# Lower shift and scale in two quarters, first two feed-forward units interleaved, nine half units parked

## The reference, cut to what matters

```python
cond = jax.nn.silu(c)
for i in range(DEPTH):
    mod = jnp.einsum('bd,sdk->bsk', cond, ada_w[i]) + ada_b[i]
    shift_t, scale_t, gate_t = jnp.split(mod[:, 0], 3, axis=-1)
    shift_m, scale_m, gate_m = jnp.split(mod[:, 1], 3, axis=-1)
    h = modulate(rmsnorm(x, norm_g[i, 0]), shift_t, scale_t)
    ...
    x = x + gate_t[:, None, :] * y
    h = modulate(rmsnorm(x, norm_g[i, 1]), shift_m, scale_m)
    x = x + gate_m[:, None, :] * sq_relu_mlp(h, mlp_w1[i], mlp_w2[i])
return rmsnorm(x, final_g)
```

## Time and profile before

| | |
|---|---|
| median of 3 runs | 2360.92 us |
| lowest, highest | 2359.98, 2361.58 us |
| span of the profiled execution | 2356.4 us |
| what lies outside the span, by the three runs | 3.6 to 5.2 us |
| PE busy, PEld busy | 2263.7 us (96%), 1826.6 us (78%) |
| DVE, ACT, POOL busy | 71%, 46%, 4% |

### The profile page before, as it was taken

One profiled execution on the slowest core, in us unless ns is written; L12 is line 12 of the kernel. 1 busy time (PEld: TensorE's weight loads), 2 busy tenths in 40 slices (PEclk: granted clock), 3 DMA queues, 4 the chain that ended last, 5 costly groups with the idle time before them and its releaser, 6 DMA issues.

```text
span 2356.4 us, 28624 instructions
## 1 busy us (share of the span) xinstructions
PE 2263.7 (96%) x10121; PEld 1826.6 (78%) x10121; DVE 1667.1 (71%) x1796; ACT 1083.2 (46%) x1340; POOL 103.2 (4%) x183
## 2 busy tenths in 40 slices
PE   5489999999999998999999999999999999999998
PEld 2147788888888887888888888887888888888887
DVE  4668888888887889767667767667877555555556
ACT  2324554544534545444444444444553453443453
POOL 0000000100100001001000001000000000000000
PEclk9699999999999999999999999999999999999999
DMA  9999988998988977867667867766897766766764
GB/s 401 415 413 399 330 300 327 373 339 273 364 303 313 343 250 248 289 222 266 217 232 234 284 220 243 258 210 211 324 339 248 241 206 196 225 211 191 231 203 154
DMA packets 272172, 650.74 MB, mean 276 GB/s; under 512 B 20712, under 2 KB 21144, under 8 KB 264992
## 3 DMA queue, kind: packets, MB, share of 16 engines
q1 hardware_dynamic: 260320, 611.92, 74.7%
q0 software_dynamic: 10816, 36.24, 4.5%
q10 hardware_dynamic: 896, 0.75, 0.1%
HBM read 631.49 MB, written 17.33 MB: 275 GB/s over the span
## 4 chain that ended last, share of the span: by engine, by line
PE 85%; DVE 4%; DMA 3%; issue 1%; ACT 1%; POOL 0%; POOLq 0%; SPq 0%; DVEq 0%; ACTq 0%
PE acc L670 83%; DMA raw<-in_mlp_w 3%; DVE w_lo L1497 1%; PE tb L785 1%; PE acc L1052 1%; ACT w_hi L1102 0%; PE score_ps L1039 0%; DMA scratch<-in_decay 0%; DVE ada_acc L1503 0%; DVE h_lo L1753 0%; DVE ev L1799 0%; PE score_ps L845 0%; DVE seg_row L1586 0%; PE tb L919 0%; DVE ada_acc L1584 0%
## 5 line engine op out<-in xcount | busy, mean ns | idle before, releaser
L1497 DVE TENSOR_TENSOR w_lo<-raw,w_hi 128x1024 fp32r<-128x1024 f32 x775 | 943.9, 1223 | 591.0 <-ACT w_hi L1102 587.4
L1102 ACT ACTIVATE w_hi<-raw 128x1024 fp32r<-128x1024 f32 x775 | 821.8, 1061 | 1118.0 <-PE acc L670 984.6
L670 PE MATMUL acc<-w_hi,h_lo 128*128 128x512 f32 x1788 | 699.2, 391 | 3.7 <-issue 1.6
L670 PE MATMUL acc<-w_hi,h_hi 128*128 128x512 f32 x1788 | 696.2, 389 | 0.0
L670 PE MATMUL acc<-w_lo,h_hi 128*128 128x512 f32 x1788 | 695.8, 389 | 0.0
L670 PE MATMUL acc<-w_hi,a_lo 128*128 128x512 f32 x1312 | 513.4, 391 | 5.6 <-DVE w_lo L1497 5.6
L670 PE MATMUL acc<-w_lo,a_hi 128*128 128x512 f32 x1312 | 511.4, 390 | 0.0
L670 PE MATMUL acc<-w_hi,a_hi 128*128 128x512 f32 x1312 | 511.4, 390 | 0.0
L670 PEld LDWEIGHTS acc<-w_hi,h_lo 128*128 128x128 f32 x1788 | 335.7, 188 | 76.8 <-issue 5.5
L670 PEld LDWEIGHTS acc<-w_hi,h_hi 128*128 128x128 f32 x1788 | 335.6, 188 | 70.0
L670 PEld LDWEIGHTS acc<-w_lo,h_hi 128*128 128x128 f32 x1788 | 335.8, 188 | 68.6
(11 more groups left out here) (193 smaller groups left out, 925.7 us busy)
## 6 DMA issues: line engine op xcount, KB each, us to landing
raw<-in_mlp_w SPq DMA_DIRECT2D x512, 512.0 KB, 4.9
ada_raw<-in_ada_w SPq DMA_DIRECT2D x248, 512.0 KB, 6.4
raw<-in_ret_w_in SPq DMA_DIRECT2D x192, 512.0 KB, 4.6
ada_early_h<-in_ada_w SPq DMA_DIRECT2D x32, 1024.0 KB, 13.1
raw<-in_ret_w_out SPq DMA_DIRECT2D x64, 512.0 KB, 4.3
ada_raw<-in_ada_w SPq DMA_DIRECT2D x16, 1024.0 KB, 12.3
square_blocks<-ev POOLq DMA_DIRECT2D x84, 128.0 KB, 5.1
ev<-square_blocks POOLq DMA_DIRECT2D x21, 512.0 KB, 6.2
```

Source lines behind the costliest of these rows:

```text
L670: mm = nc.tensor.matmul(acc[pair][t][:], l[:, CK * c + j, tok], w[:, c % RING, j, :], start=first and j == 0 and i == 0, stop=last and j = ...
L1102: nc.scalar.activation(w_hi[:, o % RING], raw[:, o % RING], ACT.Copy).then_inc(hi_ready, 1)
L1497: nc.vector.tensor_tensor(w_lo[:, o % RING], raw[:, o % RING], w_hi[:, o % RING].bitcast(F32), ALU.subtract).then_inc(lo_ready, 1)
```

## The change

1. Segment 3 comes in another order: its first 16 pieces hold shift and scale together for columns 0 to 511 (quarter 0), its last 16 the same for columns 512 to 1023 (quarter 1). A piece still has 512 KB, now as two runs of 2 KB in each row of the source where it was one of 4 KB. Quarter 0 is summed in `score_ps`, quarter 1 in `mod_ps`; each has its own copy, column and gain.
2. The first two half units are run interleaved: chunks 0 and 1 of unit 0, chunks 0 and 1 of unit 1 (all four need quarter 0 only), then chunks 2 and 3 of each. Between the first four stand PE's quarter-1 pieces, the fills 4 to 7, and the column of quarter 1.
3. `first_gate` stands ahead of PE's pieces of segment 3.
4. Nine half units are parked instead of eight; group (0, 3) begins with the upper half of the ninth. The piece counts of segment 4 between chunks are moved to suit.

```diff
-PARTS = 8
+PARTS = 9
-HALVES = {(0, 0): (0, 1, 2, 3), (0, 1): (4, 5), (0, 2): (6, 7)}
+HALVES = {(0, 0): (0, 1, 2, 3), (0, 1): (4, 5), (0, 2): (6, 7), (0, 3): (8,)}
+PAIRED = ((0, 0), (0, 1), (1, 0), (1, 1), (0, 2), (0, 3), (1, 2), (1, 3))
-    return 0 if j < RING else min(SEG, 4 + 6 * (j - RING) // 5)
+    return 0 if j < len(PAIRED) else min(SEG, 6 + 6 * (j - len(PAIRED)) // 5)
```

On SP:

```diff
+            pair_behind = {14: (0,), 15: (1,), 17: (2,), 19: (3,), 28: (4,), 30: (5,), 31: (6, 7)}
             for a in range(SEG):
                 load_early(3, a)
-                if a == 30:
-                    load_chunk(0, first_part(0))
+                for s in pair_behind.get(a, ()):
+                    i, c = PAIRED[s]
+                    load_chunk(s, pair_rows[i](c))
```

On PE:

```diff
-            shared_rows(3, 0, 4)
             first_gate()
-            shared_rows(3, 4, 16)
+            shared_rows(3, 0, 12)
             pe.wait_ge(gate_ready, 4)
             pe.wait_ge(diag_ready, 1)
-            for f in range(KT // 2 - 1):
-                norm_fill(f)
-                if f in (1, 3):
-                    shared_rows(3, 15 + f, 17 + f)
-                elif f == 5:
-                    shared_rows(3, 20, 28)
-            shared_rows(3, 28, SEG)
+            norm_fill(0)
+            norm_fill(1)
+            shared_rows(3, 12, 14)
+            norm_fill(2)
+            norm_fill(3)
+            shared_rows(3, 14, KT)
             column(score_ps)
-            norm_fill(KT // 2 - 1)
+            paired_units({0: [lambda: shared_rows(3, 16, 20)],
+                          1: [lambda: norm_fill(4), lambda: norm_fill(5), lambda: shared_rows(3, 20, 24)],
+                          2: [lambda: norm_fill(6), lambda: norm_fill(7), lambda: shared_rows(3, 24, 28)],
+                          3: [lambda: shared_rows(3, 28, SEG), lambda: column(mod_ps)]})
```

On DVE:

```diff
-            early(3, 8, 11)
             gated(2)
             gated(3)
-            early(3, 11, 16)
+            early(3, 8, 11)
             mean_square()
-            early(3, 16, 18)
             diagonals()
-            early(3, 18, SEG)
+            early(3, 11, KT)
             lo(0)
             second_hi()
             second_lo(0)
-            take_half(0)
+            take_quarter(0)
...
             second_lo(1)
+            early(3, 16, 18)
+            lo(2)
+            early(3, 18, 21)
+            lo(3)
+            early(3, 21, SEG)
+            lo(4)
+            lo(5)
+            take_quarter(1)
+            gains(slice(4, 8))
             split_h(2)
```

More of the change, by code:

```diff
@@ L519, in load_early @@
                     return
-                norm, part, half = (0, seg, a // KT) if seg < 3 else (1, a // KT, seg - 3)
                 slot, to = early_slot(seg, a)
-                sp.dma_start(to, ada_flat[norm, a % KT * P:(a % KT + 1) * P, part,
-                                          half * AW:(half + 1) * AW]).then_inc(ada_in[slot], 16)
+                here = slice(a % KT * P, (a % KT + 1) * P)
+                if seg == 3:
+                    q = a // KT
+                    sp.dma_start(to.rearrange("p (j n) -> p j n", j=2),
+                                 ada_flat[1, here, 0:2, q * NB:(q + 1) * NB]).then_inc(ada_in[slot], 16)
+                else:
+                    sp.dma_start(to, ada_flat[1, here, a // KT, AW:D]).then_inc(ada_in[slot], 16)
             def load_ada(seg, a):
@@ L662, in _, with chunk @@
             n = Count()
-            def chunk(c, lhs_hi, lhs_lo, pair, first, last, tiles=range(TT)):
+            def chunk(c, lhs_hi, lhs_lo, pair, first, last, tiles=range(TT), slot=None):
+                slot = c % RING if slot is None else slot
                 for j in range(CK):
@@ L702, in first_chunk, with half_unit @@
                         tok = slice(t * P, (t + 1) * P)
-                        mm = nc.tensor.matmul(acc[0][t][:], h_lo[:, j, tok], w_hi[:, 0, j, :], start=False, stop=False)
+                        mm = nc.tensor.matmul(acc[bank_pair(0)][t][:], h_lo[:, j, tok], w_hi[:, 0, j, :], start=False, stop=False)
                 mm.then_inc(w_used, 1)
-            def half_unit(kind, pair, after, c0, free, very_first=False):
+            def paired_units(after):
[3 more added lines that the diff above has]
+                        pe.wait_ge(evac, 4 * TT)
+                        first_chunk()
+                    else:
+                        ready_h(c)
+                        chunk(c, h_hi, h_lo, bank_pair(i), c == 0, c == HALF - 1, slot=s % RING)
+                    for hook in after.get(s, []):
+                        hook()
+                n.unit("p1")
+                n.unit("p1")
+            def half_unit(kind, pair, after, c0, free):
                 for o in range(HALF):
@@ L712, in half_unit @@
                         free()
[L713 to L717, removed]
+                    ready_h(c0 + o)
+                    chunk(c0 + o, h_hi, h_lo, pair, o == 0, o == HALF - 1)
                     for hook in after.get(o, []):
@@ L1305, in _ @@
             n.add(XA=4, U=2)
-            for f in range(KT // 2 - 1):
+            for f in range(4):
                 transposed_x(f)
             hi(0)
-            copy_rows(score_ps, 2, PE_BEFORE[4 * SEG])
+            copy_rows(score_ps, 1, PE_BEFORE[QUARTER_1], 0, 2)
             norm_second()
             norm_bank(1)
-            norm_bank(2)
             act.wait_ge(hi_ready, n.n["U"] * HALF + 2)
             hi(2)
-            norm_bank(3)
-            hi(3)
-            transposed_x(KT // 2 - 1)
-            for i in range(PARTS):
+            hi(3)
+            transposed_x(4)
+            transposed_x(5)
+            hi(4)
+            transposed_x(6)
+            transposed_x(7)
+            hi(5)
+            copy_rows(mod_ps, 1, PE_BEFORE[4 * SEG], 2, 4)
+            norm_bank(2)
+            norm_bank(3)
+            hi(6)
+            hi(7)
+            for s, (i, c) in enumerate(PAIRED):
+                if s >= RING:
+                    hi(s + LEAD)
+                if c == HALF - 1:
+                    act.wait_ge(w_used, n.n["U"] * HALF + s + 1)
+                    for t in range(TT):
+                        nc.scalar.activation(part_tile(i, t), acc[bank_pair(i)][t][:], ACT.Copy).then_inc(evac, 1)
+            n.unit("p1")
+            n.unit("p1")
+            for i in range(2, PARTS):
                 for s in range(HALF):
@@ L1326, in _ @@
                 for t in range(TT):
-                    nc.scalar.activation(part_tile(i, t), acc[i % 2][t][:], ACT.Copy).then_inc(evac, 1)
+                    nc.scalar.activation(part_tile(i, t), acc[bank_pair(i)][t][:], ACT.Copy).then_inc(evac, 1)
                 n.unit("p1")
@@ L2023, in _ @@
             second_lo(1)
+            early(3, 16, 18)
[7 more added lines that the diff above has]
+            gains(slice(4, 8))
             split_h(2)
-            lo(2)
             split_h(3)
-            lo(3)
-            for i in range(PARTS):
+            lo(6)
+            lo(7)
+            for s in range(RING, len(PAIRED)):
+                early(4, late_summed(s + LEAD - 1), late_summed(s + LEAD))
+                lo(s + LEAD)
+            n.unit("p1")
+            n.unit("p1")
+            for i in range(2, PARTS):
                 for s in range(HALF):
```

75 lines of the change are left out of this document (43 added, 32 removed).

## The result

| | before | changed |
|---|---|---|
| median of 12 runs each, same chip | 2359.79 us | 2365.15 us |
| lowest, highest | 2358.43, 2361.84 | 2363.64, 2366.65 |
| span of the profiled execution | 2356.4 us | 2364.1 us |

The ratio is 1.0023 with a 95% interval of 1.0015 to 1.0031: 5.4 us slower, between 3.5 and 7.3 us. The forecast was 2368.0 in a range of 2359 to 2373, slower by 6.9 us.

A forecast was written before the change was run, and what follows sets the result against it. The prediction took PE to bound the kernel behind the start. PE 5.9 us behind at the fifth chunk, less 1.4 for the last wait, plus 2.4 for low clock, made 6.9 us slower: 2368 us, range 2359 to 2373.

The forecast's parts named there:

- What bounds the kernel: Behind the start the kernel waits for PE, busy 60 of 60 us from 200 to 260, so only PE's lost time counts.
- the rival of the loads: Start phase: the stream of loads was the real limit, so the change is 8.3 us faster, 2352.6; chance 0.12.
- Gate first and the first fill: Ahead of the first fill: gating starts 1.84 us earlier, the fill stands at 166.0 not 169.37, PE idles 5.4 us.
- The first chunk: First chunk's matmul, behind the first column: starts at 179.1, 8.6 us earlier than before, with a 2.4 us idle time.
- The fifth chunk: Behind the second column: starts at 204.5, where it was 198.6, after a 2.9 us path; PE is 5.9 us behind.
- The clock: Low clock behind the idle times at both columns: second in full, first by half, 2.4 us lost; bounds 0 and 3.2.
- The total: Whole kernel: 5.9 - 1.4 + 2.4 = 6.9 us slower; 4.5 of it without the clock.
- DVE beside it: Before the second column: DVE's ten pieces and two low parts end at 196.4, PE wants them at 197.5; costed at nothing.
- The last wait: PE's wait for the last piece of segment 4: all 1.4 us taken back; bounds 0 and 1.4.
- 2 KB runs: Loads of segment 3: 391 GB/s against 398, 2%, landing 0.8 us later, under the slack; no cost counted.
- the first rival: At the columns: no low clock and shorter seams, 4.5 down to 2.5 us slower, 2363.4 to 2365.4; chance 0.25.
- The base: From span to median: the span lies 4.5 us below the median of the runs, so 2363.3 becomes 2367.8.

The follow-up runs named there:

- e2: The changed kernel with fills 4 and 5 moved right behind the first column, ahead of the first chunk; 2364.17 us, ratio 1.0017 to the kernel before.
- e8: The kernel before with nine half units parked instead of eight and nothing else of the change; 2358.58 us, ratio 0.9995.
- e1: The changed kernel with PE's last quarter-1 pieces and the second column ahead of chunk 1 of unit 1; 2362.72 us, ratio 1.0015 to the kernel before.
- e5: As e3, with DVE summing pieces 16 and 18 of segment 3 ahead of chunk 0's low part; 2360.58 us, ratio 1.0003 to the kernel before.
- e6: As e5, with PE's pieces 12 and 13 moved back ahead of the first fill; 2357.97 us, ratio 0.9998 to the kernel before.
- e3: The changed kernel with the edits of e1 and e2 together; 2362.2 us, ratio 1.0012 to the kernel before.
- e4: The kernel before with the gate row ahead of PE's first two pieces of segment 3, nothing else of the change; 2359.2 us, ratio 0.9999.
- e7: As e6, with piece 21 moved from DVE to PE; 2359.32 us, ratio 1.0001 to the kernel before.

## Why the prediction was right, point by point

- **What bounds the kernel: half wrong.** I read "PE busy all 60 us" as a start that waits for PE alone, and held that against the rival of the loads. The gate-first kernel shows that PE's place in that stretch is set by loads: 2.9 us won ahead of it are gone by 187.65. A busy PE and a full DMA can both be read in one window, and the chain tells which leads. It did no harm to the sign, since the changed kernel is late on PE by more than the loads leave.
- **Gate first and the first fill: right.** I put the first fill 16.2 us behind the pooling end, with 5.4 of idle time; it stood 15.6 behind, with 5.08.
- **The first chunk: right.** 29.3 us behind the pooling end by the sum, 28.4 measured, and the wait ahead of it 2.1 for 2.4.
- **The fifth chunk: right.** 204.5 by the sum, 204.71 measured; ACT's copy 0.74 for 0.75, the wait ahead of it 2.9 for 2.9. That last hit is in part luck, as 2.9 was picked between bounds of 1.3 and 3.3. The pooling end was 1.4 us earlier than in the kernel before, so the way to the fifth chunk was 1.6 us longer than I had it. That is the clock behind the first column, which the sum to this point leaves out.
- **The clock: the mis-sized term.** I counted the second column's stretch in full and the first by half, 2.4 us. Both fell. The first cost 4.6 - 3.0 = 1.6, by the first chunk here and in e2; the second 48.13 - 46.52 = 1.6. Together 3.2, the upper bound that I gave.
- **The total: closer than its terms, by luck.** The idle time grew by 3.8 us and not by 4.5, the clock cost 3.2 and not 2.4. The two errors nearly cancel: 7.0 for 6.9. The stretch grew by 7.4; the last 0.4 is not placed.
- **DVE beside it: right, with more margin than I gave it.** Its pieces ended at 194.06 and PE's sums began at 197.63, so 3.6 us and not 1; the ten pieces and two low parts took 14.6 us as summed, but began 2.4 earlier than I had it. The 10.3 us of the earlier trace rows are a median and not the most that a load takes, as I read them; DVE waited for no load there. With PE 4.8 us earlier and DVE 1.4 later, 6.2 against 3.6, the wait of 2.7 was there.
- **The last wait: right.** All of the 1.4 was taken back; the kernel before with nine parked units alone gets 1.1.
- **2 KB runs: nothing on the path, but 5% and not 2%.** The chain of the changed kernel has no load in it from 140 to 291. In the window 166:168 the changed kernel moves 386 GB/s and the gate-first kernel, with 4 KB runs, 408:

```profile
166.00:168.00 2.00, 2.00 (x11) 1.63 (x12) 0.00 (x0) 0.88 (x2) 0.00 (x0) 0.66 1.05 386
```

```profile
166.00:168.00 2.00, 2.00 (x11) 0.95 (x8) 1.16 (x1) 0.00 (x0) 0.00 (x0) 0.65 1.02 408
```

  It is the direction that the Trainium skill gives (Perfetto Trace Analysis, "DMA Optimizations"), by a twentieth and not dramatic. From 150 to 175 us it is 387 against 408.
- **The rival of the loads: its mechanism is there, its price was not.** I gave it 8.3 us, 10.9 of PE's chunks against 2.6 of loads (its neighbour, the first rival, should have gone down to 2.9 and not 2.5 slower, by its own bound of 1.3). With PE's delays nearly gone, the point is 283.57: 1.5 us earlier than before. DVE's last sum of segment 4 ends at 279.06, where it ended at 269.62 before, 9.4 later and not 2.6. I had counted two chunks of loads ahead of the last piece and overlooked that in DVE's written order it stands four chunks further back (`late_summed` starts from chunk 8 and not 4). DVE has them to do first, at 2.6 us a chunk and piece.
- **The rest of the kernel is not the same in every execution.** The profiled spans differ by 7.7 us and the points at 285 by 6.0. Of the other 1.7, 1.1 lie near 908 us, behind the retention of the first layer, which the change does not touch; the rest comes later. Windows of the changed kernel there:

```profile
908.00:910.00 2.00, 2.00 (x5) 1.62 (x6) 1.93 (x6) 1.76 (x6) 0.16 (x1) 0.52 0.75 272
910.00:912.00 2.00, 2.00 (x7) 1.53 (x6) 1.99 (x5) 0.00 (x0) 0.39 (x1) 0.63 0.86 236
```

  PE waits there in every kernel, first for 1.9 us, 3 us later for up to 1.3, and then for some 0.36, 0.33 and 0.80. The clock fell behind the later ones in the changed kernel, e2 and e8, behind the 1.9 in e1, e5 and e6, and not at all in before, e3, e4 and e7. In e5 it stays down from 892 to 899, and its span lies 5.4 above before's where its median lies 1.4 above. So the table's "between" compares the edits better than the spans do.
- **The base was off by 2.7 us.** I took what lies outside the span as 4.5, from the median of three runs. In every run since it is 1.8 or 1.9; the profiled execution was simply one of the kernel's faster ones. In 33 executions the kernel before has 20 spans from 2356.2 to 2357.4 and 13 from 2358.5 to 2362.0; in 34 others they lie from 2355.8 to 2359.9 without such a gap. Of the 2.9 us by which the predicted median was too high, 1.5 are the difference (6.9 for 5.4) and 1.1 the median of before, 2360.9 of three runs against 2359.8 of twelve; the rest is rounding. Against the stretch the sum was 0.5 too low.

**What stays open.** Why the medians show 5.4 us where the stretch shows 7.4. A part can be worked out: an early end of the pooling product gives the kernel before nothing (gate first), but a PE-bound start gains by it, so an execution of before with an end at 148.5 would read 136.5 between and not 135.2. That leaves 6.1, inside the interval of 3.5 to 7.3. No version beats the kernel before by what these runs can tell; the intervals of e4 to e8 all hold 1. The lowest runs of e5 to e8 are 2356.87, 2357.27, 2356.97 and 2356.95, against 2358.03 for the lowest of the 33 of before beside them, but 2357.59 was the lowest of before beside e1 to e4. So the 1.1 to 1.5 us by which e6, e7 and e8 reach the point at 285 earlier are read from one trace each and not shown in the times.

## What to carry to other kernels

When a stage is cut in two so that its first half can start earlier, the way from the last sum to the first product (copy, column, bias, modulation, split) is paid once for each half, and PE must have work to lay over each of them: one chunk or two fills behind the column took back 3.4 to 4.7 us here, more than half of it idle time and the rest clock. Price a new idle time of 2 us on PE together with the low clock that may stand behind it, 1.6 us a time in this kernel. And before an engine that is 100% busy is called the bound, make it earlier by a microsecond in one small edit and see if a later point moves.

## What the runs showed of the hardware

- The same idle time does not always bring the clock down. Behind 2.30 us of idle time near 141 us the window 142:144 shows 0.54 in the kernel before and 0.50 in e1, e2 and e5, but 1.00 in the six others, behind 2.28 to 2.67 us. The timelines and windows of e5 and e7:

```profile
140.98 1.94 PE L823 MATMUL mod_ps<-ada_acc,ones 128*32 128x512 f32 x8 [2.30 <-DVE ada_acc L1552]
```

```profile
142.00:144.00 2.00, 2.00 (x16) 0.23 (x8) 0.00 (x0) 0.00 (x0) 0.00 (x0) 0.50 1.05 386
```

```profile
140.89 1.07 PE L823 MATMUL mod_ps<-ada_acc,ones 128*32 128x512 f32 x8 [2.30 <-DVE ada_acc L1551]
```

```profile
142.00:144.00 2.00, 2.00 (x13) 1.05 (x6) 1.01 (x2) 0.00 (x0) 0.00 (x0) 1.00 1.05 387
```

- Eight matmuls take 1.94 us in the one and 1.07 in the other. The executions whose pooling product ends at 149.8 to 150.2 are the four in which the clock fell there; the others end at 148.5 to 148.8. Up to there the work is the same in all ten, so one execution can be some 1.0 to 1.7 us late at one place by this alone. The like is seen behind the idle time ahead of the first fill: e6 and e7 have one order of work on PE there, and their 32 records of fills took 5.43 and 6.63 us.
- The clock also fell behind 2.12 us of idle time (0.91, 0.50, 0.74 in the windows from 176 us), with 0.74 of idle time just ahead of it. That is less than the 2.30 us of idle time in the row from which I priced the clock.
